# One step of a hybrid decoder: sample scores by heads in four column groups instead of by batches in two

## The chip, the core and the metric

The kernel is one program on one core of a Trainium2 chip. The metric is the time of one execution on the device in microseconds. Everything is computed in float32. The engines named below are TensorE (PE, its weight loads PEld), VectorE (DVE), ScalarE (ACT), GpSimd (POOL) and SyncE (SP); each runs its own instruction list and they meet through semaphores.

## What is computed

One layer of a decoder runs for two groups of tokens that share the weights: a prompt of 512 tokens, and 8 samples (batches) of 4 new tokens each with a past of 512 tokens. Cut to what matters here:

```python
# per layer: x += concat(HGRN2 heads, MoBA heads) @ w_out
#            x += CrossAttn_4heads(rmsnorm(x), K/V of mem)
#            x += HierarchicalMoE(rmsnorm(x))      # 32 experts, 3 x 1024 x 1024 each
# MoBA for a sample: 8 heads of 64 features, keys from 4 pages of 128 tokens plus the 4 new ones
s = einsum('qhd,hqjsd->hqjs', q, k_pages) * MB_DIM ** -0.5 - slopes * dist
p = softmax(concat([s_pages, s_own]));  o = p @ v
# cross attention of a sample: 4 heads of 256 features over 256 cached memory rows
s = einsum('bthd,bmhd->bhtm', q, mk) * XA_DIM ** -0.5
p = softmax(s);  o = einsum('bhtm,bmhd->bthd', p, mv)
```

With 8 samples of 4 tokens, a score tile has only 4 queries for each head and sample. The keys of every sample are its own, so samples can't share a stationary operand with a moving one.

## The kernel before

The program is written out by hand, engine by engine. The order on TensorE is the order of the calls at the end of its block; results pass through seven PSUM banks in turn (class `Banks`, whose job list fixes who empties which), while bank 6 holds the sample scores. Three parts of the program matter here.

*Page stage (about 376 to 480 us).* The keys of one sample come in pages, are turned 128x128 by transposes (`keys_turned`, L2295), and copied to `kT[b % 2]` by ScalarE (chunks 0 and 2) and VectorE (chunks 1 and 3, L1309). `scores(b0)` (L2307) then multiplies two samples: for each of the four chunks of 128 features (two heads each) and each of the two samples one matmul with 32 stationary columns (`qxm[:, c, b, :]`, 8 heads x 4 tokens, zero where the chunk is not the head's) into 32 rows of bank 6. The rows of a sample are 32 x (b % 4) onward, so a call writes two of the four groups of 32 output rows. On TensorE a group of 32 output rows is a column group of the array: matmuls that write different groups can run side by side. Two calls fill the 128 rows for four samples; `new_scores(g)` (L2316) adds the scores against the new keys in a bank of its own, with four groups. VectorE adds the ALiBi table `sbias` and does the softmax over all 128 rows (`sample_probs`), the probabilities are turned (`probs_turned`, L2324 and L2327), and `sample_out(g)` (L2337, L2340) multiplies them with the value pages, four samples in four groups. Between these calls stand the output projections `rows_summed` (L2088), which cover the softmax.

*Sample cross attention (about 597 to 641 us).* The same shape with 256 memory rows and eight chunks: `mem_keys_turned(b)` (L2470), `mem_scores(b0)` (L2482, 16 matmuls of 256 columns, two samples and so two groups), softmax (`mem_probs`), `mem_probs_turned` (L2490), `mem_out` (L2500, four groups), `mem_out_turned` (L2510). The keys are loaded by GpSimd's queue into three buffers; the load for sample b waits until the transposes of sample b - 3 are done. The values of samples 4 to 7 are loaded by SP's queue behind the first `mem_out`.

*Experts (from about 733 us).* A loop over pairs of experts reads 12 MB of weights for each expert. SP's queue issues each 2 MB block when TensorE has used up the buffer that it goes to.

The queries are spread into the zeroed `qxm` by `sample_queries_apart` (L1455, on VectorE in the HGRN2 part, behind the third of its inside-weights steps) and into `qxx` by the copies at L1733. `quarters` (L2059) is a third user of four groups: 32 token rows times a weight block in quarters of 128 columns.

## Time and profile before

| | |
|---|---|
| median of 3 runs | 1689.2 us (1688.91 to 1696.76) |
| the profiled execution | 1691.88 us, its span 1688.8 us |
| TensorE busy | 1540.0 us, 91% of the span |
| DMA | 499.98 MB, mean 296 GB/s |
| the chain that ended last | TensorE 51%, DMA 39%, VectorE 6% |
| mean granted TensorE clock | 0.978 |

The span runs from the first to the last instruction in the records; the execution's time has about 3 us around it. TensorE's busy share is high because rows of pipelined matmuls overlap, so two kernels are better compared by the time from the start of one group of rows to the next. The granted clock is 1.00 at 2.4 GHz and 0.50 at 1.2 GHz. "The chain" is followed back from the last instruction, at each step to what released it.

### The profile page before, as it was taken

Reading aid. Unit: us, or ns where it says so; the run is one execution under the profiler, and the core shown is the slowest. Engines: PE = TensorE matmul, PEld = TensorE weight load, DVE = VectorE, ACT = ScalarE, POOL = GpSimd, SP = SyncE. Lnnn points to the kernel's source line nnn. Section 1 sums busy time; section 2 is a strip of 40 time slices with the busy share of each in tenths; the row PEclk is TensorE's granted clock in tenths of the full one; section 3 lists DMA queues with packets and bytes.
Section 4 is the critical chain, followed back from the end, with each engine's and each line's share of the span. In section 5 each row is a group of like instructions: output and inputs, shape, how many; then the busy total and the mean of one; then the engine's idle time right before and its main releaser. Section 6 shows DMA issues by size and latency. Waiting matters only on the chain.

```text
span 1688.8 us, 20157 instructions
## 1 busy us (share of the span) xinstructions
PE 1540.0 (91%) x8100; PEld 680.0 (40%) x8100; DVE 618.3 (37%) x1134; ACT 285.2 (17%) x646; POOL 48.4 (3%) x62
## 2 busy tenths in 40 slices
PE   7999999979999999979998899889889889888996
PEld 3444555544444664533333333333333233333332
DVE  2055775443240432543342332234233223322425
ACT  3114235342120220301000000100000010000002
POOL 3000000001010000000000000000000000000000
PEclk9999999999999999979999999999999999999999
DMA  6311220459443267369999999999999999999992
GB/s 222 141 59 50 77 100 1 152 179 337 153 163 141 75 224 321 129 239 427 427 428 428 429 428 428 427 428 427 429 428 427 428 428 428 428 428 428 428 426 94
DMA packets 69640, 499.98 MB, mean 296 GB/s; under 512 B 6912, under 2 KB 7472, under 8 KB 45008
## 3 DMA queue, kind: packets, MB, share of 16 engines
q1 hardware_dynamic: 58704, 468.47, 67.3%
q0 software_dynamic: 7760, 23.92, 4.1%
q10 hardware_dynamic: 3120, 6.82, 1.1%
q8 instruction: 38, 0.62, 0.1%
q14 instruction: 18, 0.15, 0.0%
HBM read 491.97 MB, written 11.14 MB: 298 GB/s over the span
## 4 chain that ended last, share of the span: by engine, by line
PE 51%; DMA 39%; DVE 6%; ACT 2%; issue 1%; SPq 1%; ACTq 0%; DVEq 0%; POOLq 0%
DMA ring<-w 38%; PE psum L2699 11%; PE psum L2088 11%; PE psum L2074 8%; PE psum L2638 4%; PE psum L2180 3%; PE psum L2653 1%; PE psum L2059 1%; PE psum L2307 1%; PE psum L2482 1%; DVE ring L1440 1%; PE psum L2430 1%; PE psum L2447 1%; PE psum L2228 1%; PE psum L2470 1%
## 5 line engine op out<-in xcount | busy, mean ns | idle before, releaser
L2638 PE MATMUL psum<-ring,r_c 128*64 128x512 f32 x1504 | 342.1, 602 | 29.0 <-DMA ring<-w 27.8
L2699 PE MATMUL psum<-ring,r_c 128*64 128x512 f32 x1024 | 236.7, 611 | 53.4 <-DMA ring<-w 39.3
L2638 PEld LDWEIGHTS psum<-ring,r_c 128*64 128x64 f32 x1504 | 110.6, 138 | 253.2 <-issue 192.8
L1959 DVE TENSOR_TENSOR r_x<-r_x,psum 128x1024 f32<-128x1024 f32 x64 | 78.2, 1221 | 267.9 <-PE psum L2653 267.9
L2699 PEld LDWEIGHTS psum<-ring,r_c 128*64 128x64 f32 x1024 | 77.1, 139 | 190.9 <-issue 119.4
L2074 PE MATMUL psum<-r_h,ring 128*128 128x512 f32 x320 | 140.9, 600 | 1.9 <-ACT r_h L879 1.9
L1977 DVE TENSOR_SCALAR r_c<-r_c 128x512 f32<-128x512 f32 x32 | 13.5, 422 | 299.8 <-ACT r_c L1246 299.8
L2653 PE MATMUL psum<-r_c,early 64*128 64x512 f32 x512 | 122.3, 608 | 0.8 <-ACT r_c L1253 0.8
L1246 ACT ACTIVATE r_c<-psum 128x512 f32<-128x512 f32 x32 | 19.1, 597 | 590.9 <-PE psum L2638 590.9
L2088 PE MATMUL psum<-ring,r_h 128*128 128x512 f32 x256 | 115.5, 611 | 1.0 <-DMA ring<-w_in 1.0
L1979 DVE RECIPROCAL r_c<-r_c 128x512 f32<-128x512 f32 x32 | 107.3, 3353 | 1.1
L2074 PEld LDWEIGHTS psum<-r_h,ring 128*128 128x128 f32 x320 | 60.8, 192 | 77.5 <-issue 75.3
L2653 PEld LDWEIGHTS psum<-r_c,early 64*128 64x128 f32 x512 | 46.0, 186 | 76.4 <-issue 76.4
L2088 PEld LDWEIGHTS psum<-ring,r_h 128*128 128x128 f32 x256 | 49.6, 196 | 62.1 <-issue 61.7
L1253 ACT ACTIVATE r_c<-psum 128x512 f32<-128x512 f32 x32 | 19.1, 597 | 262.9 <-PE psum L2699 262.9
L2638 PE MATMUL psum<-r_mix,r_c 128*64 128x512 f32 x256 | 58.4, 598 | 0.0
L2088 PE MATMUL psum<-ring,r_c 128*128 128x512 f32 x128 | 58.2, 600 | 0.0
L2638 PE MATMUL psum<-r_h,r_c 128*64 128x512 f32 x256 | 57.7, 593 | 0.0
L2180 PE MATMUL psum<-ring,r_h 128*128 128x512 f32 x128 | 57.0, 598 | 0.6 <-DVE r_x L1493 0.6
L2088 PE MATMUL psum<-ring,r_mix 128*128 128x512 f32 x128 | 56.8, 597 | 0.8 <-ACT r_mix L879 0.8
L844 POOL DMA_INDIRECT r_c<-tok_rows,table x16 | 17.9, 1121 | 885.7 <-PE psum L2617 775.0
L879 ACT ACTIVATE ring<-psum 128x512 f32<-128x512 f32 (+3 forms) x63 | 28.0, 531 | 65.2 <-PE psum L2088 27.8
(371 smaller groups left out, 1394.2 us busy)
## 6 DMA issues: line engine op xcount, KB each, us to landing
ring<-w SPq DMA_DIRECT2D x158, 2048.0 KB, 23.7
r_mix<-w SPq DMA_DIRECT2D x16, 2048.0 KB, 26.6
r_h<-w SPq DMA_DIRECT2D x16, 2048.0 KB, 27.4
ring<-w_in SPq DMA_DIRECT2D x6, 2048.0 KB, 9.9
ring<-cache_mem_v SPq DMA_DIRECT2D x8, 1024.0 KB, 10.3
ring<-cache_mem_k POOLq DMA_DIRECT2D x8, 1024.0 KB, 8.3
ring<-cache_moba_v SPq DMA_DIRECT2D x24, 256.0 KB, 5.4
ring<-w_xk SPq DMA_DIRECT2D x2, 2048.0 KB, 7.6
```

What stands on the lines that cost most here:

```text
L844: pool.indirect_dma_start(xg, None, tok_rows, bass.IndirectOffsetOnAxis(ap=table[:, c:c + 1], axis=0), bounds_check=TOK - 1, oob_is_err=Fa ...
L879: J.empties(act.activation(out, view(src) if view else src, ACT.Copy), *name)
L1246: act.activation(he[u], psum[2 + 2 * u], ACT.Exp, scale=-1.0).then_inc(up_exp, 1)
L1253: act.activation((late_ys if late else ys)[u], psum[7], ACT.Copy).then_inc(y_free, 1)
L1959: return dve.tensor_tensor(x, x, psum_t[:, bank:bank + 2, :].rearrange("p a n -> p (a n)"), ALU.add)
L1979: dve.reciprocal(he[u], he[u]).then_inc(dve_moe, 1)
L2074: ins = pe.matmul(s, w[:, k, P * c:P * (c + 1)], hT[:, k, 0:SEQ], start=(k == 0), stop=(k == KC - 1))
L2088: ins = pe.matmul(J.bank(*name), rows_at(lhs, i)[:, k, :], w[:, k, :], start=(k == 0), stop=(k == KC - 1))
L2180: ins = pe.matmul(J.bank("mem", n, i), memT[:, k, P * i:P * (i + 1)], w[:, k, :], start=(k == 0), stop=(k == KC - 1))
L2638: ins = pe.matmul(psum[2 + 2 * u + m][CAP * half:CAP * (half + 1), :], xT[:, k, CAP * u:CAP * (u + 1)], (first_row(2 + m, kk) if first els ...
L2653: ins = pe.matmul(psum[bank + half], of[e][rr, P * i:P * (i + 1)], src[e][rr, :], start=(e == 0), stop=(e == 1), skip_group_check=True)
L2699: ins = pe.matmul(psum[7][CAP * half:CAP * (half + 1), :], heT[u][:, k % 4, CAP * (k // 4):CAP * (k // 4 + 1)], place[:, kk, 512 * half:51 ...
```

## The change

The rows of the score tiles are laid out in another way. For the page scores, the 32 rows of column group c belong to heads 2c and 2c + 1, that is to feature chunk c, and hold all four samples: row 16 x (head % 2) + 4 x token + sample. A chunk of 128 features then goes to its own column group, and a call of `scores` visits the four groups for one sample and then for the next. The stationary operand of a sample is zero in the columns of the other samples, so samples are added up in the same rows: the first sample of four has `start`, the last has `stop`. For cross attention column group h belongs to head h (chunks 2h and 2h + 1), with 16 of its 32 rows in use. The matmuls and their shapes stay as they are in number; each chunk is now multiplied only into its own group, where before it was added into all 32 rows of its sample with zeros for the other heads.

What follows from it: the bias table `c_sbias` is permuted on the host; the queries are spread in another pattern; and since the turned probabilities now have the sample as the fastest index, the output matmuls read their 32 stationary columns four words apart (`turned[:, j, b]`), while the copy of the new tokens' turned probabilities brings them back into order. The rows of the outputs are as before for the pages, and 8 x head + token for cross attention.

```diff
-    b, h, q = p // 32, (p % 32) // NQ, p % NQ
+    b, h, q = p % 4, p // 16, p // 4 % NQ
...
-                for h in range(MB):
-                    par, c = h % 2, h // 2
-                    rr = slice(64 * par, 64 * par + 64)
-                    ins = dve.tensor_copy(qxm[rr, c, :, NQ * h:NQ * (h + 1)],
-                                          mqT[rr, c, SEQ:TOK].rearrange("p (b t) -> p b t", t=NQ))
+                for b in range(NB):
+                    for par in range(2):
+                        rr = slice(64 * par, 64 * par + 64)
+                        ins = dve.tensor_copy(qxm[rr, :, b, 16 * par:16 * par + 16].rearrange("p c (t n) -> p n c t", n=4)[:, b % 4],
+                                              mqT[rr, :, SEQ + NQ * b:SEQ + NQ * (b + 1)])
...
-                evac(ptn[0:NS, :], "Ptn", g, view=lambda s: s[0:NS, 0:P])
+                evac(ptn[0:NS, :].rearrange("p (b m) -> p b m", b=4), "Ptn", g,
+                     view=lambda s: s[0:NS, 0:P].rearrange("p (m b) -> p b m", b=4))
...
-            for h in range(XH):
-                for c in (2 * h, 2 * h + 1):
-                    ins = dve.tensor_copy(qxx[:, c, :, NQ * h:NQ * (h + 1)],
-                                          qT[:, c, SEQ:TOK].rearrange("p (b t) -> p b t", t=NQ))
+            for b in range(NB):
+                ins = dve.tensor_copy(qxx[:, :, b, 0:16].rearrange("p c (t n) -> p n c t", n=4)[:, b % 4],
+                                      qT[:, :, SEQ + NQ * b:SEQ + NQ * (b + 1)])
...
-                                                  s[:, 2 * (h % 2) + u, :, NQ * h:NQ * (h + 1)])
+                                                  s[:, 2 * (h % 2) + u, :, 8 * h:8 * h + NQ])
...
-                for c in range(4):
-                    for b in (b0, b0 + 1):
-                        ins = pe.matmul(psum[6][32 * (b % 4):32 * (b % 4) + 32, :], qxm[:, c, b, :], kT[b % 2][:, c, :],
-                                        start=(c == 0), stop=(c == 3), skip_group_check=True)
+                for b in (b0, b0 + 1):
+                    for c in range(4):
+                        ins = pe.matmul(psum[6][32 * c:32 * c + 32, :], qxm[:, c, b, :], kT[b % 2][:, c, :],
+                                        start=(b % 4 == 0), stop=(b % 4 == 3), skip_group_check=True)
...
-                        ins = pe.matmul(s[32 * b:32 * b + 32, :], ptS[:, j, 32 * b:32 * b + 32], vbuf[b][:, j, :],
+                        ins = pe.matmul(s[32 * b:32 * b + 32, :], turned[:, j, b], vbuf[b][:, j, :],
...
-                for c in range(KC):
-                    for b in (b0, b0 + 1):
-                        ins = pe.matmul(psum[6][32 * (b % 4):32 * (b % 4) + 32, 0:MEM], qxx[:, c, b, :], xkT[b % 2][:, c, :],
-                                        start=(c == 0), stop=(c == KC - 1), skip_group_check=True)
+                for b in (b0, b0 + 1):
+                    for u in range(2):
+                        for h in range(XH):
+                            ins = pe.matmul(psum[6][32 * h:32 * h + 32, 0:MEM], qxx[:, 2 * h + u, b, :], xkT[b % 2][:, 2 * h + u, :],
+                                            start=(b % 4 == 0 and u == 0), stop=(b % 4 == 3 and u == 1), skip_group_check=True)
```

`new_scores` and `mem_out` change in the same way as `scores` and `sample_out`. On TensorE the instructions of the page stage stand in the same order and number. Here are the second score call with the new scores behind it, and the turned probabilities (names: output tile, then inputs by buffer; shape of the output; a minus is before, a plus after):

```order
 L2307 MATMUL psum<-ring 32x512 x8
-L2316 MATMUL psum<-r_c,ring 32x32 x16
+L2315 MATMUL psum<-r_c,ring 32x32 x16
 L2088 MATMUL psum<-ring,r_mix 128x512 x8
 L2295 MATMUL psum<-ident,r_c 128x128 x16
-L2324 MATMUL psum<-ident,r_c 128x128 x4
-L2327 MATMUL psum<-ident,r_c 32x128
+L2323 MATMUL psum<-ident,r_c 128x128 x4
+L2326 MATMUL psum<-ident,r_c 32x128
```

Nothing moved but line numbers; what changes inside a row is the group of output rows that each matmul of it writes, in turn 0, 1, 0, 1 before and 0, 1, 2, 3 now for the first of these calls' rows, and which sample and chunk it reads.

On VectorE the one place with another count is in the HGRN2 part, between the masked copies of the second head and the gate of the third (L1371), which ScalarE waits for:

```order
 L1433 COPY_PREDICATED atts<-masks,psum 32x32
 L1451 MEMSET ring 128x1024
-L1455 COPY ring<-r_c 64x8x4 x8
+L1455 COPY ring<-r_c 64x4x4 x16
 L1371 TENSOR_SCALAR r_c<-r_c,omlb,lb 128x544
 L1373 TENSOR_SCALAR r_c<-r_c 128x544
```

Eight copies of 32 elements for each partition became sixteen of 16. ScalarE's list is the same, and so are those of SP and GpSimd but for line numbers.

## Rows read from the trace of the kernel before

**Rows 1.** The page: its span, and the chain that ended last, shares by engine.
```profile
span 1688.8 us, 20157 instructions
...
PE 51%; DMA 39%; DVE 6%; ACT 2%; issue 1%; SPq 1%; ACTq 0%; DVEq 0%; POOLq 0%
```

**Rows 2.** Chain in time (start us, us); stretch: busy by engine, clock, DMA share, GB/s.
```profile
1033.77 25.12 DMA ring<-w
...
1000.00:1600.00 600.00, 539.44 (x2730) 195.51 (x2728) 186.18 (x195) 46.02 (x100) 10.20 (x9) 0.99 1.01 428
```

**Rows 3.** Chain in time, page stage: start us, us, engine, line, rows.
```profile
400.75 3.56 PE psum L2307 x16
...
415.88 1.97 PE psum L2307 x9
...
419.50 0.26 PE psum L2316 x21
...
431.91 3.57 PE psum L2340 x32
...
458.01 2.34 PE psum L2088 x5
```

**Rows 4.** Chain in time, cross attention of the samples, and one line's wait.
```profile
602.45 3.60 PE psum L2482 x32
...
615.06 3.64 PE psum L2500 x32
...
635.88 5.34 PE psum L2500 x32
...
608.80 3.65 PE L2482 MATMUL psum<-r_h,ring 128*32 128x256 f32 x32 [0.87 <-DVE r_h L1309]
```

**Rows 5.** Stretch 452 to 456 us; and TensorE in order of time, with its wait.
```profile
452.00:456.00 4.00, 3.54 (x14) 1.00 (x16) 0.32 (x1) 0.00 (x0) 0.00 (x0) 0.57 0.02 4
...
452.46 1.07 PE L2307 MATMUL psum<-ring 128*32 128x512 f32 x2 [2.28 <-DVE ring L1309]
```

**Rows 6.** Chain in time; and the weight loads of its line (ns min/median/max).
```profile
669.76 3.68 PE psum L2059 x128
...
L2059 PEld LDWEIGHTS psum<-ring,r_c x128: 106/110/110, 669.7 to 673.0; 128*32 128x32 f32 x128
```

**Rows 7.** Issues and their user in order of time; issues of three stretches, us to landing.
```profile
428.74 1.88 SPq L632 DMA_DIRECT2D r_c<-cache_moba_k  x4
...
448.22 1.97 PE L2295 MATMUL psum<-ident,r_c 128*128 128x128 f32 x16
...
599.26 0.70 POOL L831 DMA_DIRECT2D ring<-cache_mem_k  x1 [100.24 <-PE psum L2470]
...
601.00 0.71 POOL L831 DMA_DIRECT2D ring<-cache_mem_k  x1 [1.04 <-PE psum L2470]
...
ring<-cache_mem_k POOLq DMA_DIRECT2D x1, 1024.0 KB, 5.1
...
ring<-cache_mem_k POOLq DMA_DIRECT2D x1, 1024.0 KB, 7.9
...
ring<-cache_mem_v SPq DMA_DIRECT2D x2, 1024.0 KB, 11.4
```

**Rows 8.** Weight loads of transposes, side by side and with a step; a run.
```profile
L2295 PEld LDWEIGHTS psum<-ident,r_c x48: 138/140/142, 386.9 to 449.8; 128*128 128x128 f32 x48
...
L2617 PEld LDWEIGHTS psum<-ident,r_c x128: 195/211/226, 730.4 to 1593.1; 128*128 128x128 f32 x128
...
821.74 1.23 PE L2617 MATMUL psum<-ident,r_c 128*128 128x128 f32 x8
```

**Rows 9.** VectorE and ScalarE in order of time, third head.
```profile
182.42 1.50 DVE L1455 COPY ring<-r_c 64x32 f32<-64x32 f32 x8
...
183.96 0.56 DVE L1371 TENSOR_SCALAR r_c<-r_c,omlb,lb 128x544 f32<-128x544 f32 x1
...
189.26 0.66 ACT L935 ACTIVATE ring<-r_c 128x544 f32<-128x544 f32 x1
```

More of the change, by code:

```diff
@@ L2312, in new_scores @@
                 J.wait_free(pe, "Sn", g)
-                for c in range(4):
-                    for b in range(4 * g, 4 * g + 4):
-                        q = slice(32 * (b % 4), 32 * (b % 4) + 32)
-                        ins = pe.matmul(J.bank("Sn", g)[q, 0:NS], qxm[:, c, b, :], mkT[:, c, SEQ:TOK], start=(c == 0),
-                                        stop=(c == 3), skip_group_check=True)
+                for b in range(4 * g, 4 * g + 4):
+                    for c in range(4):
+                        ins = pe.matmul(J.bank("Sn", g)[32 * c:32 * c + 32, 0:NS], qxm[:, c, b, :], mkT[:, c, SEQ:TOK],
+                                        start=(b % 4 == 0), stop=(b % 4 == 3), skip_group_check=True)
                 J.fills(ins, "Sn", g)
@@ L2334, in sample_out @@
                 pe.wait_ge(v_in, 16 * NPG * 4 * (g + 1))
+                turned = ptS.rearrange("p j (m b) -> p j b m", b=4)
                 s = J.bank("Os", g)
@@ L2495, in mem_out @@
                 pe.wait_ge(xv_in, 16 * 4 * (g + 1))
+                turned = xptS.rearrange("p j (m b) -> p j b m", b=4)
                 for half in range(2):
@@ L2499, in mem_out @@
                         for b in range(4):
-                            ins = pe.matmul(J.bank("XOs", g, half)[32 * b:32 * b + 32, :], xptS[:, j, 32 * b:32 * b + 32],
+                            ins = pe.matmul(J.bank("XOs", g, half)[32 * b:32 * b + 32, :], turned[:, j, b],
                                             xvbuf[b][:, j, 512 * half:512 * (half + 1)], start=(j == 0), stop=(j == MT - 1),
```

## The prediction

> **What bounds the kernel now.** I read the summary of the chain first: half of the span stands under TensorE and 39% under the DMA of the expert weights [rows 1]. The chain in order of time then splits the program. Behind 830 us it is a stream of weights: 25.12 us of DMA and a short run of matmuls, again and again, and the stretch table has the DMA engines at share 1.01 and 428 GB/s there [rows 2]. What starts that stream is TensorE (each weight buffer is asked for when the matmuls before it are done), so the end moves with the time at which TensorE reaches the experts, and the stream itself is no shorter or longer. Ahead of it TensorE is the engine on the chain, and both stages that the change touches lie there: 400 to 458 us for the page scores, 602 to 636 us for sample cross attention.
>
> In these the reader should look at the time per matmul, not at the count. Every fp32 matmul leaves two rows. A call of page scores (L2307) is 8 matmuls, 16 rows of 512 columns, and takes 3.56 us, 0.22 us a row; L2340 has 32 rows of the same shape in 3.57 us, 0.11 us a row [rows 3]. The only difference is the number of column groups in turn, two for L2307 and four for L2340. The scores of cross attention (L2482) are 32 rows of 256 columns in 3.60 to 3.65 us (the first two of four calls) [rows 4], again two groups. So half the array stands idle in eight calls: L2307 at 400.75, 415.88, 444.73 and 452.46, L2482 at 602.45, 608.80, 623.22 and 629.57 us.
>
> **The change, part by part.** *Page scores.* After it a call visits four groups, so 16 rows take half of what L2340 needs for 32: 3.57 / 2 = 1.79 us. The calls at 400.75 and at 444.73 save 3.56 - 1.79 = 1.77 us each. The second call runs with the new-token scores (L2316) behind it, part of them slipped into its idle groups: 3.88 us from 415.88 to the end of the new scores at 419.76 [rows 3]. After the change nothing can slip in; I take 1.79 us and 0.4 us for the 32 small rows (21 of them took 0.26 us at the end of the call) = 2.2 us, 1.65 us less. The fourth call takes 5.55 us for the same work, from 452.46 [rows 5] to the projection at 458.01 [rows 3], since the granted clock averages 0.57 from 452 to 456 us, which is 1.2 GHz for 3.44 of the 4 us, behind 2.28 us in which TensorE had waited for VectorE's copies of the last keys [rows 5]. That wait stays: it runs from the end of the third call over copies that the change doesn't touch. If the clock comes back at the same distance (455.44, 3.0 us behind the call's start), 1.5 us of the 2.2 us are done by then and the call takes 3.0 + 0.7 = 3.7 us, 1.85 us less. Sum: 1.77 + 1.65 + 1.77 + 1.85 = 7.0 us.
>
> *Cross attention scores.* No row of before has 256 columns in four groups. The bounds: the row of 128 columns in four groups, 128 rows in 3.68 us or 0.029 us each [rows 6], says that issue and weight loads stand in nobody's way, and the call halves to 1.83 us, 1.78 us less. The other end is no gain, if the loads of 32 columns, 0.110 us each [rows 6] where the call now has a row each 0.112 us, had to run one behind the other. That 0.110 us is read from L2059 itself, which has a row each 0.029 us, so its loads overlap, and I take the halving: 4 x 1.78 = 7.1 us.
>
> *What is late next.* The keys of cross attention are the nearest. The DMA of batch 3 is issued at 599.26 us, when the transposes of batch 0 are done, and lands 5.1 us later; batch 4 is issued at 601.00 and lands 7.9 us later, at 608.9 [rows 7]. Neither issue moves, since the transposes ahead of the first score call don't. TensorE now wants batch 3 at 605.96 and batch 4 at 612.4; after it, at 604.2 and 608.8. So batch 3 is 0.2 us late, or 0.9 us if the count runs from the end of the issue; most of that goes into the 0.87 us that TensorE stands before the next scores anyway, for VectorE's copies [rows 4]. Batch 4 is 0.1 to 0.8 us late, and there nothing covers it. I take 0.3 us off. The values of batches 4 to 7, issued behind the first output, land some 11.4 us later [rows 7], near 631; they shift by two calls to 627.4, and the second output wants them at 635.88 - 7.1 = 628.8. That is 1.3 us of margin, nothing off. In the page stage the margins are wide: the last keys are issued at 428.74 and wanted 19.5 us later, at 448.22 [rows 7]; the change takes 1.8 us from that.
>
> *Weights read with a step.* The matmuls with the probabilities (L2340, L2500: 64 rows each) now read a stationary operand of 32 columns that stand four words apart. The bound from the trace: the expert stage's transposes load every fourth column, 0.211 us a load against 0.140 us for columns side by side, and a run of eight takes 1.23 us [rows 8], the last one's own 0.28 us within it: 0.95 / 7 = 0.136 us each. L2295's sixteen take 1.97 us [rows 7], 1.70 / 15 = 0.113 us each. A gain has no reason here, so the lower end is 0. The upper end is 0.07 us for each round of four groups that isn't hidden: 128 / 4 x 0.07 = 2.3 us. In L2340 a round lasts 0.43 us and the load is over long before, so I take 0. The Trainium skill (SBUF — State Buffer, in the section on Door 1) speaks against this edit: consecutive accesses run at full rate only with at least two hits in a 16-byte line, and four fp32 words are a full line. By that rule each of the 32 columns pays; the longer load of the transposes agrees with it, and the sum would be 2.3 us worse only if nothing hid the load.
>
> *VectorE.* The copies that spread the page queries (L1455) become 16 of half the size: 8 take 1.50 us now, so at most 1.5 us more. Behind them stands L1371, which ScalarE's logarithm wants at 189.26 us and which ends at 184.5 us [rows 9]. 4.7 us of cover, cost nothing; without it the chain would grow by 1.5 us. The copies of the cross queries (L1733) stay eight of the same size. The turned copy of the new probabilities and the last copies of the outputs keep count and size. Nothing moves on the DMA queues, no wait is added, and the instruction counts on TensorE are the same.
>
> **Sum.** 7.0 + 7.1 - 0.3 = 13.8 us. The profiled execution took 1691.9 us with a span of 1688.8 us, so its like would be a span of 1675.0 us; the median of the runs shown is 1689.2 us, and 1689.2 - 13.8 = 1675.4 us.
>
> **Rivals.**
> *The loads of the cross scores are the bound.* For it: a load of 0.110 us for each 0.112 us now. Against: L2059. Then only the page part remains: 1689.2 - 7.0 = 1682.2 us.
> *Less of the gain arrives.* Late keys at their worst (0.5 us more), loads with a step in the open (2.3 us), and one more stretch at the low clock, worth the 5.34 - 3.64 = 1.7 us by which the second run of L2500 is longer than the first [rows 4]: 13.8 - 4.5 = 9.3 us, 1679.9 us. In the other direction both low stretches can vanish, since the work around them changes: 1.5 us in the fourth call and 1.7 us in L2500, 17.0 us in all, 1672.2 us. The rows of before don't say which.
> *The gain is given back.* The scores finish earlier and TensorE waits for a copy or a DMA instead: about 1689 us. Against it: five of the eight calls are followed at once by work whose operands are there, two by the transposes whose keys are late by the amounts above, and the softmax behind the eighth keeps its length.
> *Slower.* The loads with a step stand in front of their matmuls, one behind the other over the groups, 128 times. At the full 0.211 us of a load with a step this costs 27 us: 1689.2 + 27.0 - 13.8 = 1702.4 us. It decides from 13.8 / 128 = 0.11 us for each load. Against it: in the expert stage such transposes follow each other every 0.136 us though their loads show 0.211 us, so even 128 columns overlap.
> *The change doesn't do what it says.* If sums of several batches into the same rows held the four groups in order, a call would keep its 3.6 us and the time 1689 us. But the sums over feature chunks do the same now, in L2340 too, and run in four groups.
>
> **How the numbers follow.** The forecast, with its own spread of 1672 to 1680 us, has 0.82; loads as the bound 0.07; given back, or no groups in parallel, 0.06; a partial gain beyond 1680 us 0.03, most of it still below 1680.8; slower 0.02. The range that leaves out 2 in 10 reaches from both low stretches gone to the loads as the bound: 1671.5 to 1682.5 us. A measurement of this kernel can tell about 0.5%, 8.4 us, from no change. Faster than 1680.8 us: 0.84. Within: 0.14. Slower: 0.02.
>
> **What would show it.** In the changed kernel's chain the calls of page scores should stand with about 1.8 us for 16 rows, those of cross scores with about 1.8 us for 32 rows; 3.6 us for the latter and half for the former is the first rival. L2340 and L2500 (moved down a line or two) should keep 3.6 us; more, with TensorE's weight loads longer than 0.110 us, is the load with a step. A wait for the cross keys before the transposes of batches 3 and 4 would be the late DMA. The first output of the experts should come 13.8 us earlier, with 428 GB/s behind it and the same distance to the end. The prediction is wrong if that distance grows, or if the score calls halve and the experts don't start earlier.

## The result

The changed kernel takes 1676.8 us (median of 8 runs, 1672.0 to 1681.9), the kernel before 1688.9 us in the same job (8 runs, 1687.3 to 1696.8). The ratio is 0.9923, with a 95% interval of 0.9909 to 0.9938: 12.1 us less on these medians, where 13.8 us had been forecast. The profiled execution of the changed kernel took 1672.02 us with a span of 1670.2 us, the shortest of its eight, so its span is 18.6 us below the profiled span of before and must not be read as the gain. The other 6.5 us are treated in the section on both kernels a second time.

**What bounds it now.** The head of the page, which answers to [rows 1]: nearly the same division (TensorE 50% where it had 51%), 18.6 us shorter.

```profile
span 1670.2 us, 20165 instructions
...
PE 50%; DMA 40%; DVE 6%; ACT 2%; issue 1%; SPq 1%; ACTq 0%; DVEq 0%; POOLq 0%
```

**The page stage**, by the chain in order of time (start us, us, engine, what, rows). It answers to [rows 3].

```profile
396.72 1.75 PE psum L2295 x16
398.47 1.85 PE psum L2307 x16
...
411.90 1.91 PE psum L2307 x14
413.81 0.30 PE psum L2315 x30
...
441.04 1.29 DVE ring L1309 x2
...
445.03 0.14 issue
445.17 1.91 PE psum L2307 x14
447.07 0.30 PE psum L2315 x29
```

Score calls (L2307) stand with 1.85 and 1.91 us where they had 3.56 us. The new-token scores (L2315) no longer slip into gaps of the call but follow it with 0.30 us. The fourth call, which ran at the low clock before and took 5.55 us with the new scores [rows 3, 5], takes 2.21 us here, and there is no low-clock stretch: the granted clock from 440 to 456 us is 1.00, where 452 to 456 us had 0.57.

**Cross attention of the samples**, the same view; it answers to [rows 4].

```profile
586.32 1.76 PE psum L2470 x16
588.08 0.29 issue
588.37 5.30 DMA ring<-cache_mem_k
593.67 0.04 issue
593.72 1.98 PE psum L2470 x16
595.70 0.02 issue
595.72 0.70 DVE r_h L1309
596.42 0.14 issue
596.56 1.93 PE psum L2483 x32
598.49 1.90 PE psum L2470 x16
...
609.32 1.91 PE psum L2483 x32
...
613.95 1.97 PE psum L2483 x32
...
618.58 3.67 PE psum L2502 x32
```

The calls (L2483) take 1.91 to 1.97 us instead of 3.60 to 3.66. A new step stands on the chain: behind the first transposes (L2470) it no longer goes through the first score call (1.93 us from 591.49, off the chain) but through the DMA of the next keys. The second output call (L2502) has 3.67 us, where L2500 had 5.34 at the low clock.

**The experts.** The first row is the first expert matmul of the chain; the other is the stretch from 1000 to 1600 us (us; busy by engine; granted clock; DMA share; GB/s), as in [rows 2].

```profile
715.30 16.30 PE psum L2640 x64
```

```profile
1000.00:1600.00 600.00, 542.35 (x2744) 197.04 (x2740) 183.10 (x190) 46.02 (x100) 10.19 (x9) 0.99 1.01 428
```

The experts start at 715.30 us, where they had started at 733.59, and the stream behind runs at 428 GB/s as before. From there to the end of the span it is 954.9 us, against 955.2: what TensorE gained ahead of the experts arrived at the end.

**Splitting the 18.3 us.** The stage that the change touches runs from the first page transposes (399.00 us before, 396.72 after) to the first expert matmul. It lasted 334.6 us and lasts 318.6, 16.0 us less; the other 2.3 us lie ahead of it, where nothing was changed but the copies of L1455, which are not on the chain. Of the 16.0 us the stretches at the low clock are a part, and the experiments below treat that part apart.

### The profile page after: what moved, and what is told of

It is laid out like the page before. It is cut to its first block, busy times and chain, and to the rows that moved or that the text cites. A ratio compares the mean times of both kernels' runs of the same rounds, so it can differ in the third digit from the quotient of the medians.

```text
span 1670.2 us, 20165 instructions
## 1 busy us (share of the span) xinstructions
PE 1522.2 (91%) x8100; PEld 675.0 (40%) x8100; DVE 619.8 (37%) x1142; ACT 284.8 (17%) x646; POOL 48.3 (3%) x62
## 4 chain that ended last, share of the span: by engine, by line
PE 50%; DMA 40%; DVE 6%; ACT 2%; issue 1%; SPq 1%; ACTq 0%; DVEq 0%; POOLq 0%
DMA ring<-w 38%; PE psum L2701 11%; PE psum L2088 11%; PE psum L2074 8%; PE psum L2640 4%; PE psum L2180 3%; PE psum L2655 1%; PE psum L2059 1%; DVE ring L1440 1%; PE psum L2430 1%; PE psum L2447 1%; PE psum L2228 1%; DMA ring<-w_in 1%; PE psum L2106 1%; PE psum L2209 1%
## 5 line engine op out<-in xcount | busy, mean ns | idle before, releaser
L2074 PE MATMUL psum<-r_h,ring 128*128 128x512 f32 x320 | 140.6, 600 | 1.9 <-ACT r_h L879 1.9
L2088 PE MATMUL psum<-ring,r_h 128*128 128x512 f32 x256 | 114.0, 605 | 1.0 <-DMA ring<-w_in 1.0
L2074 PEld LDWEIGHTS psum<-r_h,ring 128*128 128x128 f32 x320 | 61.0, 192 | 77.1 <-issue 74.9
L2088 PEld LDWEIGHTS psum<-ring,r_h 128*128 128x128 f32 x256 | 49.0, 194 | 61.1 <-issue 60.1
L2088 PE MATMUL psum<-ring,r_c 128*128 128x512 f32 x128 | 58.2, 600 | 0.0
L2088 PE MATMUL psum<-ring,r_mix 128*128 128x512 f32 x128 | 56.8, 597 | 0.8 <-ACT r_mix L879 0.8
```

The lines of the kernel that those rows point to most:

```text
L2074: ins = pe.matmul(s, w[:, k, P * c:P * (c + 1)], hT[:, k, 0:SEQ], start=(k == 0), stop=(k == KC - 1))
L2088: ins = pe.matmul(J.bank(*name), rows_at(lhs, i)[:, k, :], w[:, k, :], start=(k == 0), stop=(k == KC - 1))
```

## Experiments

In all of them the measure beside the time is the length of this stage, from the first page transposes to the first expert matmul.

### Only the page scores

The layout of `qxm`, `scores`, `new_scores`, the bias and the page outputs as in the changed kernel; cross attention as before.

```diff
-                for b in (b0, b0 + 1):
-                    for u in range(2):
-                        for h in range(XH):
-                            ins = pe.matmul(psum[6][32 * h:32 * h + 32, 0:MEM], qxx[:, 2 * h + u, b, :], ...
+                for c in range(KC):
+                    for b in (b0, b0 + 1):
+                        ins = pe.matmul(psum[6][32 * (b % 4):32 * (b % 4) + 32, 0:MEM], qxx[:, c, b, :], ...
```

> The changed kernel with the cross attention part undone: page scores in four groups, cross attention scores in two. Theory (each score call halves because four groups run side by side, and the stream behind carries the gain to the end): four page calls of 1.8 to 1.9 us for 16 rows instead of 3.6, 7.0 us off the kernel before, and 8.4 us where the fourth call has no stretch at the low clock, so a ratio of 0.995 to 0.996. Rival (the gain is mostly the low-clock stretches that vanished, not the halved calls): the third call still takes 3.6 us or its 1.7 us are given back before the experts, and the ratio is above 0.998.

Measured: 1682.4 us (1680.5 to 1689.4, 12 runs) against 1689.2; ratio 0.9962 [0.9945, 0.9978]. Chain in order of time of this kernel:

```profile
441.23 1.90 PE psum L2308 x16
...
595.25 3.60 PE psum L2483 x32
...
628.69 5.34 PE psum L2501 x32
```

The page calls have halved, the cross calls have not, and the low clock in the second output call is still there. 6.8 us less, where the sum had 7.0.

### Only the cross scores

The counterpart: the kernel before, with the cross part of the change.

```diff
-                for c in range(KC):
-                    for b in (b0, b0 + 1):
-                        ins = pe.matmul(psum[6][32 * (b % 4):32 * (b % 4) + 32, 0:MEM], qxx[:, c, b, :], ...
+                for b in (b0, b0 + 1):
+                    for u in range(2):
+                        for h in range(XH):
+                            ins = pe.matmul(psum[6][32 * h:32 * h + 32, 0:MEM], qxx[:, 2 * h + u, b, :], ...
```

> The kernel before with the cross attention part alone. Theory: four calls of cross attention scores of 1.9 us for 32 rows instead of 3.6, with 0.3 to 0.5 us lost to the keys of batch 3, which land at the same distance from the transposes of batch 0: 6.3 to 6.8 us off, ratio 0.996. The two parts then add up to the 13 us of the whole change. Rival (the weight loads of 0.110 us bind at 256 columns): no call below 3.5 us and a ratio of 1.000. Second rival (the parts share a gain, such as one low-clock stretch that either removes): both parts together give more than 15 us.

Measured: 1683.8 us (1680.6 to 1689.9, 12 runs); ratio 0.9966 [0.9950, 0.9983], 5.4 us less where the sum had 6.8. Chain in order of time:

```profile
444.55 3.56 PE psum L2306 x16
...
452.29 3.58 PE psum L2306 x9
...
599.02 5.27 DMA ring<-cache_mem_k
...
619.93 1.91 PE psum L2482 x32
```

The page calls are as in [rows 3], with the fourth at the low clock as in [rows 5]; the cross calls have halved, and the DMA of the keys stands on the chain here too, so it belongs to this half. The two halves together are 12.2 us, the whole 12.1 (and 13.0 by its ratio): they add up within what these medians can tell.

### Groups in runs

The same matmuls into the same rows, in an order that stays longer in one column group: runs of 4 rows in the page calls, of 8 rows in the cross calls, where the changed kernel takes another group with every matmul (2 rows).

```diff
-                for b in (b0, b0 + 1):
-                    for c in range(4):
+                for c in range(4):
+                    for b in (b0, b0 + 1):
...
-                for b in (b0, b0 + 1):
-                    for u in range(2):
-                        for h in range(XH):
+                for h in range(XH):
+                    for b in (b0, b0 + 1):
+                        for u in range(2):
```

> The changed kernel with another order inside a score call: all matmuls of a column group in a row (page: two samples, 4 rows of the profile for each group; cross attention: 8 rows), then the next group. Same matmuls, same groups, same sums. If TensorE starts its matmuls strictly in the order of the program, a group's rows run one behind the other and only its last one overlaps the next group's first: 4 x 3 x 0.43 + 0.43 = 5.6 us for a page call and 4 x 7 x 0.215 + 0.215 = 6.2 us for a cross call instead of 1.9 each, 32 us in all, a ratio to the kernel before of 1.01. If it looks ahead past a waiting group (in the kernel before rows of the new scores start between rows of page scores that stand ahead of them in the program), the calls stay at 1.9 to 2.4 us and the ratio at 0.992 to 0.994.

Measured: 1687.6 us (1684.4 to 1693.5, 12 runs); ratio 0.9992 [0.9974, 1.0009]. Chain in order of time:

```profile
400.48 1.88 PE psum L2307 x16
...
447.28 1.91 PE psum L2307 x14
...
595.13 4.54 PE psum L2483 x32
```

This is neither of the two cases as they were written: strict order had 5.6 and 6.2 us for a call, look-ahead 1.9 to 2.4 us. In runs of 4 rows the calls keep their 1.88 to 1.95 us; in runs of 8 rows they take 4.54 to 4.58 us, 0.142 us a row, which is longer than the two groups in turn of before (0.113 us a row, [rows 4]). So rows for another group do start ahead of a row that waits for its own group, but only over a short distance. Between the two stages the length of the run differs, and the shape too, which the next experiment separates.

That matmuls start out of turn is to be seen in the kernel before, too. TensorE in order of time there, in the second page call, where all the rows of L2307 stand ahead of those of L2316 in the program (start us, us, line, rows):

```profile
415.88 2.34 PE L2307 MATMUL psum<-ring 128*32 128x512 f32 x10 [0.87 <-DVE ring L1309]
417.63 0.26 PE L2316 MATMUL psum<-r_c,ring 128*32 128x32 f32 x4
418.02 1.05 PE L2307 MATMUL psum<-ring 128*32 128x512 f32 x4
```

Trainium skill, TensorE: Matmul & The Clock Gate, "The mechanism" of packing small matmuls: matmuls start and end in program order there, without reordering. These rows speak against it as a general rule, and the measurement decides: rows of L2316 started at 417.63 us, ahead of rows of L2307 at 418.02. If strict order held, a page call in runs of 4 rows would have taken the 5.6 us of the expectation; it took 1.88 us.

### Runs of four rows in the cross calls

```diff
-                    for u in range(2):
-                        for h in range(XH):
+                    for h in range(XH):
+                        for u in range(2):
```

> The changed kernel with the two feature chunks of a head one behind the other in the cross attention scores: 4 rows of the profile for each column group in a run instead of 2, where runs of 8 rows took 4.54 us a call. If TensorE's look past a waiting group is limited by the number of rows that wait, then 4 rows, which were free in the page calls, are free here: 1.9 to 2.0 us for 32 rows. If it is limited by the time for which a group is busy (4 rows of 256 columns are half as long as 4 of 512), 1.9 us as well and no more than the page calls show. Against both: anything above 2.4 us would mean that the number of rows in the call, 32 instead of 16, is what made the runs of 8 slow.

Measured: 1676.5 us (one run). Chain in order of time:

```profile
600.03 1.97 PE psum L2483 x32
```

1.96 to 2.01 us, as with a change of group at every matmul. It is the length of the run that costs, not the 256 columns. And the length counts in rows, not in time: with two groups in turn a group takes a row of 512 columns every 0.44 us and one of 256 every 0.23 us (twice the times per row of [rows 3] and [rows 4]), so that a run of 4 page rows and a run of 8 cross rows keep their group busy for about 1.8 us each, and only the second costs. That is an estimate from these rows; which limit stands behind it isn't shown. For this change it means that the gain hangs on the order of the loops: with the groups outermost the four cross calls take 18.2 us, where before they took 14.5.

### Columns side by side

To price the step in the stationary operand: the copies of the turned probabilities out of PSUM put the samples back in order, and L2339 and L2500 load 32 adjacent columns as before.

```diff
-                evac(ptS, "Pt", g, view=lambda s: s.rearrange("p (j n) -> p j n", j=NPG))
+                evac(ptS.rearrange("p j (b m) -> p j b m", b=4), "Pt", g,
+                     view=lambda s: s.rearrange("p (j m b) -> p j b m", j=NPG, b=4))
...
-                        ins = pe.matmul(s[32 * b:32 * b + 32, :], turned[:, j, b], vbuf ...
+                        ins = pe.matmul(s[32 * b:32 * b + 32, :], ptS[:, j, 32 * b:32 * b + 32], vbuf ...
```

> The changed kernel, but ScalarE's copies of the turned probabilities put each sample's 32 columns side by side, so that the 128 output matmul rows load their weights without a step; ScalarE now reads PSUM with a step instead. Theory (the longer loads of 0.136 us instead of 0.110 are hidden behind rounds of 0.43 us): the output calls stay at 3.6 us and the time is that of the changed kernel within 1 us, ratio 0.992 to 0.993. Rival (a load with a step costs time in the open): 1 to 2.3 us less, ratio 0.991 or below. ScalarE's copies stand ahead of the output matmuls with 0.5 us of TensorE idle in two of the four places, so each 0.1 us by which they grow costs 0.2 us.

Measured: 1675.6 us (1671.4 to 1677.1, 6 runs); ratio 0.9914 [0.9888, 0.9939], the changed kernel within its interval. The weight loads of the output line, in the changed kernel and here (ns min/median/max):

```profile
L2340 PEld LDWEIGHTS psum<-ring,r_c x48: 134/136/159, 426.2 to 465.5; 128*32 128x32 f32 x48
```

```profile
L2339 PEld LDWEIGHTS psum<-ring,r_c x48: 106/110/110, 423.0 to 462.2; 128*32 128x32 f32 x48
```

Reading four words apart makes a load of 32 columns 136 ns instead of 110. The call of 32 rows takes 3.60 us with the one (at 426.26 us in the changed kernel's chain) and 3.57 with the other: the load is over long before its group is free. Trainium skill, SBUF — State Buffer, on Door 1: the rule that accesses with less than two hits in a 16-byte line don't run at the full rate agrees in the sign, and the price is 26 ns a load, all but 0.03 us of it hidden.

### Both kernels a second time

The gap between the profiled span (-18.6 us) and the medians (-12.1 us) asked whether the stretches at the low clock belong to a kernel or to an execution. Both kernels, unchanged:

> The changed kernel again, unchanged, for a second profile. What is asked is where the stretches at the lower clock fall. If they follow from the kernel's own order, this profile shows them as the first did: none in the fourth page call, one of 3.4 us near 492, and none in the second cross output call (3.6 to 3.7 us). If they vary from execution to execution, the stretch near 492 may be 6.8 us long and the second output call 5.3 to 5.4 us, as in the kernel with the page change alone. The sample calls stay at 1.85 to 1.97 either way.

> The kernel before again, unchanged, for a second profile. If the stretches at the lower clock follow from the kernel's order: near 452 (3.4 us, inside the fourth page call, then 5.5 us instead of 3.6), near 505 and near 638 (inside the second cross output call, 5.34 us), as in the first profile. If they vary from execution to execution, at least one of the three is elsewhere or has another length.

Measured: 1675.4 us and 1689.7 us (one run each). The stretch table of the two (us; busy and instructions of TensorE, weight loads, VectorE, ScalarE, GpSimd; granted clock; DMA share; GB/s), and the changed kernel's fourth page call by the chain. The kernel before:

```profile
450.00:456.00 6.00, 4.14 (x16) 1.15 (x18) 1.66 (x5) 0.00 (x0) 0.00 (x0) 0.72 0.01 3
502.00:508.00 6.00, 6.00 (x11) 2.49 (x12) 1.15 (x1) 0.00 (x0) 0.00 (x0) 0.72 1.03 408
636.00:640.00 4.00, 4.00 (x28) 0.99 (x20) 0.00 (x0) 0.60 (x1) 0.00 (x0) 0.57 0.02 4
```

The changed kernel:

```profile
446.00:450.00 4.00, 3.75 (x48) 1.43 (x48) 0.18 (x2) 0.00 (x0) 0.00 (x0) 0.57 0.01 4
494.00:498.00 4.00, 3.35 (x5) 1.56 (x6) 1.72 (x4) 0.60 (x2) 0.00 (x0) 0.57 1.02 409
614.00:630.00 16.00, 12.57 (x94) 6.41 (x93) 5.33 (x13) 3.49 (x8) 0.00 (x0) 1.00 0.59 224
```

```profile
446.25 3.59 PE psum L2307 x14
449.83 0.31 PE psum L2315 x29
```

A clock of 0.57 over 4 us, or 0.72 over 6, is 3.4 us at 1.2 GHz, and costs some 1.7 us (the second output call: 5.34 against 3.64 us, [rows 4]; the fourth page call with its new scores: 3.90 against 2.21 us). The kernel before has the same three in both profiles. The changed kernel has one in its first profile (490 to 496 us) and two in its second, one of them in the fourth page call, which then takes 3.59 + 0.31 = 3.9 us. They vary from execution to execution, and the disappearance of the stretch near 452 is no fixed effect of the change. With each 3.4 us counted as 1.7 us, the stage gives one picture over fourteen profiles:

| Kernel | Stage, us | 3.4-us low stretches, 390 to 690 us | Without them, us |
|---|---|---|---|
| before | 334.6 | 3 | 329.5 |
| before, again | 334.5 | 3 | 329.4 |
| only the page scores | 327.6 | 3 | 322.5 |
| only the cross scores | 328.6 | 3 | 323.5 |
| groups in runs | 331.0 | 3 | 325.9 |
| changed | 318.6 | 1 | 316.9 |
| changed, again | 319.6 | 2 | 316.2 |
| columns side by side | 320.8 | 3 | 315.7 |
| runs of four | 321.1 | 3 | 316.0 |
| keys on SyncE's queue | 321.1 | 3 | 316.0 |
| page order | 316.1 | 1 | 314.4 |
| cross order | 318.2 | 3 | 313.1 |
| both orders | 312.4 | 0 | 312.4 |
| both orders, keys on SyncE | 313.1 | 1 | 311.4 |

The rows "changed" to "keys on SyncE's queue" have the same score calls and average 316.2 us: the change is worth 13.3 us of stage, the page part alone 7.0 and the cross part alone 6.0. The rest between executions is the low clock and the noise ahead of the stage. The correction is my reckoning from rows, not a measurement, and 1.7 us is a little too much for the stretch near 492 us. The projections it falls on (L2074 in the changed kernel) take 14.00 us in the profile without a stretch, 15.4 to 15.7 us with one and 16.9 to 17.0 us with the double one, so 1.4 to 1.7 us and 2.9 to 3.0 us. With what each profile shows there, the change is worth 13.0 us, the page part 6.6 and the cross part 6.0: the last column is good to 0.5 us or, for a single profile, 1 us.

### The keys on SyncE's queue

The cross keys of batches 3 to 7 are issued on SyncE's queue instead of GpSimd's; buffers and the condition for issue stay.

```diff
+            for b in range(3, NB):
+                J.wait_filled(sp, "XKT", b - 3, 3)
+                sp.dma_start(xkbuf[b % 3], a["cache_mem_k"][0][b] ...).then_inc(xk_late_in[b % 3], 16)
...
-            for b in range(NB):
-                if b >= 3:
-                    J.wait_filled(pool, "XKT", b - 3, 3)
+            for b in range(3):
                 pool.dma_start(xkbuf ...
```

> The changed kernel, with the cross keys of batches 3 to 7 loaded by SyncE's hardware queue instead of GpSimd's software queue; the first three batches and all else stay. In the changed kernel's profile the transposes of batch 3 stand behind a wait for the keys' transfer of 5.30 us (588.37 to 593.67), which cost 0.43 us of what the first cross call had been expected to give. Theory (the transfer binds, and its start on GpSimd's queue is part of it): the transfer lands 0.3 to 0.5 us earlier, the transposes of batch 3 start by 593.4 or so counted from the same place, some 0.3 to 0.4 us of the wait goes, and the total is 1676.4, which no timing of this kernel can tell from 1676.8; the verdict is the chain's row. Rival (the bandwidth of the filled queues binds, whatever queue issues): the transfer still takes 5.2 to 5.4 us to land and the wait stays. Second rival (SyncE's queue is in order and has streamed weights in front of the keys): the keys land later than before and the first cross call comes 1 us later or more.

Measured: 1676.8 us (1675.0 to 1677.7, 4 runs); ratio 0.9928 [0.9911, 0.9944], no difference from the changed kernel. Chain in order of time:

```profile
589.74 1.76 PE psum L2476 x16
591.52 5.44 DMA ring<-cache_mem_k
597.01 1.98 PE psum L2476 x16
```

The theory holds for the start: the 0.29 us between the end of the transposes and the issue is gone. The rival holds for the rest: the transfer takes 5.44 us, where the profiles with GpSimd's queue have 5.2 to 5.4. From the first transposes to the end of the second score call it is 12.04 us, against 12.17 and 12.05 in the two profiles of the changed kernel. A gain of 0.3 to 0.4 us isn't seen there, nor could the totals have shown it.

### Other work into the waits

What is left in both stages after the change is waiting for softmax and for copies; before the fourth page call TensorE waits from 441.02 to 445.17 us. Three kernels put projections there that don't depend on it: in the page stage the first projection of the second half (`rows_summed(1, 0)`, L2088) goes ahead of `scores(6)`, and the turning of the probabilities goes inside the next one; in cross attention the first block of `x2` goes behind the last `mem_scores`, and the turning of its probabilities goes inside it. The first edit alone, the second alone, and both:

```diff
+            rows_summed(1, 0)
             scores(6)
             new_scores(1)
-            rows_summed(1, 0)
-            probs_turned(1)
-            rows_summed(1, 1)
+            rows_summed(1, 1, {5: lambda: probs_turned(1)})
```

```diff
             mem_scores(6)
-            mem_probs_turned(1)
+            rows_of(("x2", 0, 0), 0, weights("xo0"), oT, {3: lambda: mem_probs_turned(1)})
             mem_out(1)
```

> The changed kernel with TensorE's first projection of the second half (sample-free rows 0) moved ahead of the fourth page score call, and the turning of the probabilities moved inside the next projection. Theory (behind the halved calls TensorE now stands 2.3 us for VectorE's copies of the last keys, with nothing to do): that wait falls under the projection and the time drops by 2.3 us, ratio to the kernel before 0.991. Rival (the wait only moves: the projection that covered it is missing as cover of the softmax or of VectorE's row sums): a wait of 1 us or more in front of the turned probabilities or of the sample output, and less than 1 us of gain.

> The changed kernel with the first output projection of cross attention (prompt rows 0) moved ahead of the second sample output, the turning of the last probabilities inside it, and the second projection ahead of the turned outputs. Theory: the 1.7 us and 0.5 us that TensorE stands behind the last score call for the softmax go, 2.2 us. If the low clock that followed that idle time in five of the six profiles (output call 5.34 instead of 3.64 us) is caused by it, the output call stays at 3.6 us in the profile and another 1.7 us go, 3.9 us in all: ratio 0.990. Rival (the low clock has nothing to do with that idle time): the output call still takes over 5 us and the gain is 2.2 us, ratio 0.991.

> Both moves on the changed kernel. Theory: they add up, 4.5 us less than the changed kernel, 6.2 us where the low-clock stretch behind the cross scores goes too: ratio to the kernel before 0.9885 to 0.990. Rival (the experts' start is held by something else once TensorE is earlier, such as the gather or the first blocks of weights): the score stages end 4.5 us earlier and the first expert matmul doesn't.

Measured: 1672.7 us (1671.3 to 1675.9; 0.9908 [0.9891, 0.9924]), 1673.7 us (1669.4 to 1673.8; 0.9899 [0.9882, 0.9915]) and 1667.6 us (1666.4 to 1670.4; 0.9874 [0.9858, 0.9891]), 4 runs each. Chain in order of time of the kernel with both, and its stretch table around the fourth call:

```profile
443.20 1.90 PE psum L2301 x16
445.09 6.87 PE psum L2094 x16
451.96 1.85 PE psum L2313 x16
```

```profile
440.00:456.00 16.00, 16.00 (x114) 8.09 (x113) 6.05 (x16) 2.61 (x5) 0.00 (x0) 1.00 0.35 128
```

The copies of the last keys now run beside 6.87 us of projections, and the fourth call follows at once; TensorE is busy for 16.00 of the 16 us. By the medians the edits bring 4.1, 3.1 and 9.2 us against the changed kernel, where 2.3, 2.2 to 3.9 and 4.5 to 6.2 us had been expected. What the order alone brings is read from the chains between the same calls. From the third page call to the end of the second page output it is 27.39 us in the changed kernel (439.12 to 466.51) and 25.04 us with both edits, 2.4 us less. From the third cross call to the end of the second output and 7.07 us of projections it is 20.00 us (609.32 to 629.32) and 17.46 us, 2.5 us less. Together they are 4.9 us, and another 1.3 us between these two profiles is the stretch near 492 us; that makes the 6.2 us between their stages (318.6 and 312.4). The corrected lengths of the table, 1.8, 3.1 and 3.8 us below 316.2, differ from the 2.4, 2.5 and 4.9 us of the chains by 0.6, 0.6 and 1.1 us, which is as much as the length of a single profile can be off.

The rest of the 9.2 us is in part the low clock: over the whole span the mean granted clock of the four runs with both edits is 0.978 to 0.984, that of the changed kernel's eight runs 0.974 to 0.979. Whether the filled waits cause that can be counted over the fourteen profiles. There are two calls with such a wait in front, the fourth page call and the second cross output call. Where the wait was open, 13 of these 22 calls ran in part at the low clock; where an edit had filled it, none of 6 did. Chain in order of time: the cross output call of the kernel with the cross edit alone, and the projections near 492 us of the one with both edits, which have no stretch either:

```profile
629.51 3.60 PE psum L2508 x32
```

```profile
491.75 14.00 PE psum L2080 x32
```

This speaks for the waits as a cause, but doesn't show it: the same output call also kept the full clock in three profiles with its wait open (the changed kernel's two and the page edit alone), and the cross edit alone has its three stretches elsewhere, one in the fourth page call and a double one near 500 us.

A last kernel has both orders and the keys on SyncE's queue.

> Both reorderings (sums of the new rows ahead of the last score call of the page stage; sums of the first new row's block ahead of the turning of the cross probabilities) together with the cross keys of batches 3 to 7 on SyncE's queue. With the reorderings alone 1667.6 us. If the keys' wait of about 0.4 us goes, 1667.2; if the keys come later on SyncE's queue, 1668.5 or more; no more than the reorderings alone can be told from it by time.

Measured: 1672.0 us (1667.3 to 1678.6, 4 runs); ratio 0.9911 [0.9877, 0.9944]. In this profile no wait for the keys is left on the chain, all three transposes run through (L2481, 5.24 us for 48 rows from 586.33), and from the first of them to the end of the second score call it is 11.81 us instead of 12.17. That is 0.36 us, as expected (0.3 to 0.4), but the total is if anything longer and its runs spread by 11 us, so it is no version to prefer. The kernel with both orders is the best one: 9.2 us below the changed kernel's median.

## Why the prediction came out right

**Size and sign.** 1675.4 us forecast, 1676.8 measured, within the likeliest case. It rested on all three low stretches staying and the calls halving. The sum was 13.8 us of stage; the stage gives 13.0 to 13.3. The medians give 12.1 us, and how near the forecast's 1675.4 us they come is in part luck: of the five profiles with the same score calls one has a single low stretch, one has two and three have three, each worth 1.4 to 1.7 us.

**The page calls, 7.0 us.** Right in mechanism and nearly in size: the page part alone shortens the stage by 7.0 us and the median by 6.8. By single calls it is 1.71, 1.67 and 1.68 us for the first three (3.56 - 1.85, 3.88 - 2.21, 3.58 - 1.90) and 1.65 us for the fourth where it runs at the low clock in both kernels (5.55 - 3.90), 6.7 us in all; in the stage of the page part alone some 0.4 us come from the low clock, since its double stretch costs 2.97 us in the projections (16.97 - 14.00) where the two of before cost 3.37 (1.67 in the fourth call, 1.70 in the projections). The fourth was put at 3.7 us with the low clock; the second profile of the changed kernel has it so, with 3.9 us, and the first, without, has 2.2. One difference in the sum is off, 3.88 - 2.2 is 1.68 us and not 1.65, which changes nothing.

**The cross calls, 7.1 us.** The mechanism was right, the term too large. The halving of a 256-column call was an assumption between two bounds, with no row of its shape; the calls take 1.91 to 1.97 us, not 1.80 to 1.83, so four calls give 6.7 to 6.8 us. The first rival, loads of 0.110 us one behind the other, would have kept 3.6 us and is out: 32 rows in 1.93 us are 0.060 us each, little more than half a load.

**The late keys, 0.3 us.** Here a step failed. The reasoning was that batch 3, 0.2 to 0.9 us late, would disappear in the 0.87 us that TensorE waits for VectorE's copies anyway, and that batch 4 had no such cover. The chain of the changed kernel shows the opposite. The copies (L1309 at 595.72 us) follow the transposes of batch 3 and so move with them: the wait in front of L2483 is still 0.88 us, and the DMA's delay stands in series with it. Batch 4's transposes at 598.49 us follow the score call with no gap. The price is 0.36 us for batch 3 (12.17 - 11.81, the kernel without that wait) and nothing for batch 4: the total of the term was right by luck, its place wrong. With the longer calls the cross part is 6.0 us of stage instead of 6.8.

**The loads with a step, 0 us.** Right: 136 ns a load, 3.60 us a call against 3.57, and no difference in the total with adjacent columns. The slower rival, which needed 0.11 us for each of 128 loads in the open, is out.

**The copies of L1455.** Sixteen of 176 ns each, 3.03 us where eight, of 176 ns too, took 1.50: half the elements cost the same per copy, so the 1.5 us more are the upper bound that had been set. VectorE in order of time in the changed kernel, which answers to [rows 9]:

```profile
183.22 3.03 DVE L1455 COPY ring<-r_c 64x16 f32<-64x16 f32 x16
186.28 0.56 DVE L1371 TENSOR_SCALAR r_c<-r_c,omlb,lb 128x544 f32<-128x544 f32 x1
```

L1371 ends at 186.84 us, and ScalarE's activation (L935) starts at 190.06: 3.2 us of cover are left of 4.7. With the old copies the page transposes start at 398.82 us (cross scores only), with the new ones at 398.85 (page scores only). The term is nothing, as said.

**The low clock.** "The rows of before don't say which" was the right answer for the wrong quantity: it isn't the change that decides but, in the changed kernel, the execution. Single executions therefore spread more than one profile suggests: the changed kernel's runs reach from 1672.0 to 1681.9 us.

**What follows the stage.** As said: the distance from the first expert matmul to the end changed by 0.3 us, and the stream kept 428 GB/s.

## What to carry to other kernels

When fp32 matmuls have 32 output columns, as here, the time is set by how many column groups the rows near each other in the queue go to: give neighbouring matmuls different groups, by summing samples into shared rows with zeroed weights if that's what it takes, and keep the loop over the groups innermost. Before putting a delay under an existing wait, ask what that wait is for: a wait for something that itself follows the delayed work covers nothing. And compare single profiles only with the low-clock stretches counted on both sides; here they were worth some 3.7 of the 18.6 us between two spans (two stretches fewer, and a third that costs 1.4 instead of 1.7 us).

## What the runs showed of the hardware

- Rows for another column group start ahead of a row that waits for its own, but only over a short distance: runs of 4 rows cost nothing (1.97 us for a call of 256 columns, 1.88 us for one of 512), runs of 8 rows make the call 4.54 us, more than two groups in turn (3.60 us).
- A VectorE copy of 64 partitions takes 176 ns with 16 elements and 176 ns with 32; they follow each other every 0.19 us (3.03 us for 16, 1.50 us for 8, [rows 9]). At these two sizes the number of copies counts, not their size.
- A load of 32 fp32 columns takes 136 ns with a step of four words and 110 ns without.
- Between 390 and 690 us the stretches at 1.2 GHz were 3.4 or 6.8 us long in the thirteen profiles of fourteen that have any; in the kernel before they fell on the same three places in two executions, in the changed one on one place in one execution and on two in the other. In the page-only profile, the one at 492 us is twice as long (0.57 over 8 us) while the fourth page call has none. Of the fourth page calls and second cross output calls, none of 6 whose wait had been filled had one, and 13 of 22 whose wait was open did. What sets the place is open.
- The 1 MB of keys of batch 3 takes 5.2 to 5.4 us to land from GpSimd's queue (eight profiles) and 5.4 us from SyncE's (one); the issue itself is 0.70 us on the one and 0.37 us on the other.
